# Joining the first and sixth block products of a half pair to 512 columns, and ordering each joined slot

## What is computed

```python
D_MODEL = 2048; SEQ = 512; DIFF_HEADS = 8; DIFF_QK_DIM = 128; DIFF_V_DIM = 256

def diff_attention(u, w_in, w_out, lam_q1, lam_k1, lam_q2, lam_k2, subln_g, rel_table, layer_idx):
    proj = u @ w_in                                   # 512 x 2048 by 2048 x 8192: q | k | v | z
    q = split_heads(proj[..., :E], 2 * DIFF_HEADS)
    k = split_heads(proj[..., E:2 * E], 2 * DIFF_HEADS)
    v = split_heads(proj[..., 2 * E:3 * E], DIFF_HEADS)
    z = proj[..., 3 * E:4 * E]
    ...
    logits = q k^T * scale + rel_bias, causal
    p = softmax(logits);  a = p[:, :, 0] - lam * p[:, :, 1];  o = a v
    o = rms_norm(o, subln_g) * (1.0 - lam_init)
    return (o * silu(z)) @ w_out

h = layer_norm(alpha * x + diff_attention(x, ...), g, b)
```

## Time and profile before

| | us |
|---|---|
| median of 3 runs | 882.47 |
| lowest and highest | 881.83 and 882.64 |
| the profiled execution, device time | 882.91 |
| its span in the trace | 881.1 |

### The profile page before, as it was taken

How to read it: one execution, slowest core, us unless ns; L and a number is a source line. 1 busy time by engine, 2 the same in 40 slices (tenths; PEclk the granted TensorE clock), 3 DMA queues, 4 the chain that set the end, 5 groups by cost and what they waited for, 6 DMA issues and landing times.

```text
span 881.1 us, 15146 instructions
## 1 busy us (share of the span) xinstructions
PE 874.6 (99%) x5498; PEld 792.8 (90%) x5498; DVE 688.1 (78%) x1030; ACT 455.1 (52%) x695; POOL 283.6 (32%) x496
## 2 busy tenths in 40 slices
PE   9999999999999999999999999999999999999997
PEld 7888899999999999999999999999999988888886
DVE  5676778886887788778877887779777976876976
ACT  4445555545555555455545555555455662665511
POOL 1301516152505250525152515250525125130033
PEclk9999999999999999999999999999999999999999
DMA  8822686776677667857785778576857774997723
GB/s 308 312 74 79 142 222 114 225 176 191 126 228 169 179 145 229 162 166 155 232 153 165 163 224 166 156 161 198 166 158 161 259 260 133 232 180 255 286 102 113
DMA packets 54092, 161.38 MB, mean 183 GB/s; under 512 B 9760, under 2 KB 11808, under 8 KB 53808
## 3 DMA queue, kind: packets, MB, share of 16 engines
q0 software_dynamic: 24928, 71.37, 39.6%
q1 hardware_dynamic: 24720, 80.49, 25.9%
q10 hardware_dynamic: 4416, 9.18, 2.9%
HBM read 143.66 MB, written 13.15 MB: 178 GB/s over the span
## 4 chain that ended last, share of the span: by engine, by line
PE 96%; DVE 2%; DMA 0%; ACT 0%; issue 0%; SPq 0%; DVEq 0%; ACTq 0%
PE proj L1736 50%; PE att L1736 46%; DMA w_raw<-w_in_tiles_dram 0%; DVE w_split L1152 0%; DVE w_split L1168 0%; DVE scratch L1320 0%; DVE big L1728 0%; DVE scratch L1347 0%; ACT scratch L893 0%; DVE scratch L1303 0%; DVE xg_split L1465 0%; DVE scratch L1340 0%; DVE last_stats L1714 0%; DVE proj L1254 0%; DVE operands L1298 0%
## 5 line engine op out<-in xcount | busy, mean ns | idle before, releaser
L791 ACT ACTIVATE w_split<-w_raw 128x1024 fp32r<-128x1024 f32 x196 | 207.3, 1058 | 185.8 <-PE proj L1736 115.8
L1152 DVE TENSOR_TENSOR w_split<-w_raw,w_split 128x1024 fp32r<-128x1024 f32 x196 | 238.8, 1221 | 70.8 <-ACT w_split L791 69.7
L1736 PE MATMUL att<-w_split,xg_split 128*128 128x512 f32 x832 | 171.7, 362 | 0.0
L1736 PEld LDWEIGHTS att<-w_split,xg_split 128*128 128x128 f32 x832 | 140.7, 188 | 24.8
L681 POOL DMA_DIRECT2D scratch<-scratch x256 | 127.7, 594 | 41.6 <-DVE scratch L1347 32.2
L1736 PE MATMUL proj<-w_split,xg_split 128*128 128x256 f32 (+1 forms) x912 | 138.5, 311 | 0.1
L1736 PEld LDWEIGHTS proj<-w_split,xg_split 128*128 128x128 f32 x912 | 126.4, 188 | 10.1 <-DVE operands L1298 0.6
L1736 PE MATMUL proj<-xg_split,w_split 128*128 128x256 f32 (+1 forms) x864 | 128.2, 308 | 0.4 <-DVE w_split L1485 0.4
L1736 PEld LDWEIGHTS proj<-xg_split,w_split 128*128 128x128 f32 x864 | 118.3, 189 | 8.7 <-issue 0.7
L704 POOL DMA_DIRECT2D w_raw<-w_in_tiles_dram x84 | 73.9, 887 | 140.2 <-DVE w_split L1152 113.2
L1736 PE MATMUL proj<-w_split,sums 128*128 128x256 f32 (+1 forms) x768 | 104.7, 296 | 0.0
(11 more groups left out here) (188 smaller groups left out, 996.3 us busy)
## 6 DMA issues: line engine op xcount, KB each, us to landing
w_raw<-w_in_tiles_dram SPq DMA_DIRECT2D x98, 512.0 KB, 4.3
w_raw<-w_in_tiles_dram POOLq DMA_DIRECT2D x84, 512.0 KB, 5.5
w_raw<-w_out_tiles_dram SPq DMA_DIRECT2D x19, 512.0 KB, 3.7
w_raw<-w_out_tiles_dram POOLq DMA_DIRECT2D x12, 512.0 KB, 8.0
bias_by_distance<-bias_lines POOLq DMA_DIRECT2D x8, 640.0 KB, 6.2
scratch<-scratch POOLq DMA_DIRECT2D x128, 40.0 KB, 2.8
bias<-bias_by_distance POOLq DMA_DIRECT2D x8, 512.0 KB, 4.2
scratch<-scratch POOLq DMA_DIRECT2D x128, 32.0 KB, 1.7
```

Of the source, the lines that this page charges most:

```text
L791: nc.scalar.activation(split_view(a, 0), pair_raw(a), ACT.Copy).then_inc(w_hi, 1)
L1152: nc.vector.tensor_tensor(split_view(a, 1), pair_raw(a), split_view(a, 0).bitcast(F32), ALU.subtract).then_inc(w_ready, 1)
L1736: return nc.tensor.matmul(dst, lhsT, rhs, start=start, stop=stop, skip_group_check=True)
```

## The change

Steps 0 and 3 are joined too, in both halves. They use both row parts of the two `proj` banks of their column (`half_banks(h, 0)`). ScalarE no longer copies the whole of step 0 but its high-by-low half (`take_first_low`), and VectorE adds the other half to it (`keep_first`). `keep_sum` becomes two additions, the second waiting for the first. Step 6 now opens a sum of its own, so `finish_lower` adds the kept step 0 to it first, and two consumers wait for that. The new ScalarE copy has one more wait, as `kept_first` is now read until the end of a half. In all joined slots, old and new, the eight matmuls of 512 columns are issued first and the eight of 256 after them.

```diff
+        first_low = sem("first_low")
+        sum_begun = sem("sum_begun")
+        upper_left_done = sem("upper_left_done")
...
-        def wide_banks(step):
+        def wide_banks(h, step):
+            if step in (0, 3):
+                return half_banks(h, 0)
             return att[:, WIDE[step]:WIDE[step] + 2].rearrange("p b (l n) -> p b l n", l=2)
...
-            if c == 1:
+            if c == 1 and i in X_ROOM:
                 return xg_split[:, :, X_ROOM[i] + kk, HALF_SEQ:SEQ]
-            low, high, width = k * SEQ + at, D * ST + i * QE + kk * HALF_SEQ, D * ST + 4 * QE
-            return bass.AP(sums, low, [[width, P], [high - low, 2], [1, HALF_SEQ]])
+            low, width = k * SEQ + at, D * ST + 4 * QE
+            if c == 0:
+                high = D * ST + i * QE + kk * HALF_SEQ
+            else:
+                freed = SUM_AT[FREED[i]]
+                high = (2 * SK + SK * (freed % 2) + kk) * SEQ + (HALF_SEQ if freed >= 2 else 0)
+            return bass.AP(sums, min(low, high), [[width, P], [abs(high - low), 2], [1, HALF_SEQ]])
...
-            def keep_first(p, h):
+            def take_first_low(p, h):

                 act.wait_ge(quarter_done, slots_before(p) + h * PHASE + BLOCKS)
-                nc.scalar.activation(kept_first, region_of(h, 0), ACT.Copy).then_inc(first_kept, 1)
+                act.wait_ge(*((v_moved, 2 * p) if h == 0 else (lower_done, phase_number(p, 0) + 1)))
+                nc.scalar.activation(kept_first, wide_banks(h, 0)[:, :, 1], ACT.Copy).then_inc(first_low, 1)
...
             def qk_head(p, e):

                 act.wait_ge(corner_done if e == 1 else lower_done, phase_number(p, 0) + 1)
+                if e == 0:
+                    act.wait_ge(upper_left_done, phase_number(p, 0) + 1)
...
             def v_halves(p):

                 act.wait_ge(scores_done, p * ST + ST)
+                act.wait_ge(upper_left_done, phase_number(p, 1) + 1)
                 act.wait_ge(lower_done, phase_number(p, 1) + 1)
...
-                nc.vector.tensor_tensor(kept_sum, region_of(h, 3), kept_first, ALU.add).then_inc(sum_kept, 1)
+                nc.vector.tensor_tensor(kept_sum, wide_banks(h, 3)[:, :, 0], kept_first, ALU.add).then_inc(sum_begun, 1)
+                dve.wait_ge(sum_begun, n)
+                nc.vector.tensor_tensor(kept_sum, wide_banks(h, 3)[:, :, 1], kept_sum, ALU.add).then_inc(sum_kept, 1)
+
+            def keep_first(p, h):
+
+                dve.wait_ge(first_low, phase_number(p, h) + 1)
+                nc.vector.tensor_tensor(kept_first, wide_banks(h, 0)[:, :, 0], kept_first, ALU.add).then_inc(first_kept, 1)
...
                 dve.wait_ge(lower_begun, phase_number(p, h) + 1)
                 dve.wait_ge(quarter_done, slots_before(p) + (h + 1) * PHASE)
-                nc.vector.tensor_tensor(region_of(h, 5), wide_banks(5)[:, :, 1], kept_sum, ALU.add).then_inc(lower_done, 1)
+                nc.vector.tensor_tensor(region_of(h, 6), region_of(h, 6), kept_first, ALU.add).then_inc(upper_left_done, 1)
+                nc.vector.tensor_tensor(region_of(h, 5), wide_banks(h, 5)[:, :, 1], kept_sum, ALU.add).then_inc(lower_done, 1)
...
                 if j == PHASE:
                     qk_head(p, 0)
+                if r == BLOCKS:
+                    keep_first(p, h)
...
-                opens = c == 0 and (step in (0, 4) or wide)
+                opens = c == 0 and step in (4, 6)
...
+                if wide:
+                    cells = [(group, kk) for group in range(2) for kk in range(SK)]
+                    for group, kk in cells:
+                        part, opening = slice(group * P, (group + 1) * P), c == 0 and kk == 0
+                        dst = wide_banks(h, step)[:, group]
+                        if h == 0:
+                            mm(dst, w[0][:, kk, part], both_x(step, c, kk), opening, False)
+                        else:
+                            mm(dst, xs[0][:, kk, part], both_w[:, :, kk], opening, False)
+                    for group, kk in cells:
+                        part, final = slice(group * P, (group + 1) * P), c == BLOCKS - 1 and kk == SK - 1
+                        dst = wide_banks(h, step)[:, group, 0]
+                        if h == 0:
+                            last = mm(dst, w[1][:, kk, part], xs[0][:, kk], False, final)
+                        else:
+                            last = mm(dst, xs[1][:, kk, part], w[0][:, kk], False, final)
...
-WIDE = {1: 2, 2: 0, 5: 0}
+WIDE = {0: None, 1: 2, 2: 0, 3: None, 5: 0}
```

More of the change, by code:

```diff
@@ L982, in slot @@
                 if r == BLOCKS:
-                    keep_first(p, h)
+                    take_first_low(p, h)
                 late_steps(p - 1, j)
@@ L1211, in keep_sum @@
                 dve.wait_ge(quarter_done, slots_before(p) + h * PHASE + 4 * BLOCKS)
-                nc.vector.tensor_tensor(kept_sum, region_of(h, 3), kept_first, ALU.add).then_inc(sum_kept, 1)
+                nc.vector.tensor_tensor(kept_sum, wide_banks(h, 3)[:, :, 0], kept_first, ALU.add).then_inc(sum_begun, 1)
[4 more added lines that the diff above has]
+                nc.vector.tensor_tensor(kept_first, wide_banks(h, 0)[:, :, 0], kept_first, ALU.add).then_inc(first_kept, 1)
             def keep_third(p, h):
                 dve.wait_ge(third_low, phase_number(p, h) + 1)
-                nc.vector.tensor_tensor(kept_third, wide_banks(1)[:, :, 0], kept_third, ALU.add).then_inc(third_kept, 1)
+                nc.vector.tensor_tensor(kept_third, wide_banks(h, 1)[:, :, 0], kept_third, ALU.add).then_inc(third_kept, 1)
             def keep_fifth(p, h):
                 dve.wait_ge(fifth_low, phase_number(p, h) + 1)
-                nc.vector.tensor_tensor(kept_fifth, wide_banks(2)[:, :, 0], kept_fifth, ALU.add).then_inc(fifth_kept, 1)
+                nc.vector.tensor_tensor(kept_fifth, wide_banks(h, 2)[:, :, 0], kept_fifth, ALU.add).then_inc(fifth_kept, 1)
             def less_sum(p, h):
@@ L1247, in begin_lower @@
                 dve.wait_ge(quarter_done, slots_before(p) + h * PHASE + 6 * BLOCKS)
-                nc.vector.tensor_tensor(kept_sum, wide_banks(5)[:, :, 0], kept_sum, ALU.add).then_inc(lower_begun, 1)
+                nc.vector.tensor_tensor(kept_sum, wide_banks(h, 5)[:, :, 0], kept_sum, ALU.add).then_inc(lower_begun, 1)
             def finish_lower(p, h):
@@ L1855, in product @@
                             last = mm(dst, w[1][:, kk, part], xs[0][:, kk], False, final)
                         else:
-                            mm(dst, xs[0][:, kk, part], w[0][:, kk], first, False)
-                            mm(dst, xs[0][:, kk, part], w[1][:, kk], False, False)
                             last = mm(dst, xs[1][:, kk, part], w[0][:, kk], False, final)
+                else:
+                    for group in range(2):
+                        dst = region_of(h, step)[:, group]
+                        part = slice(group * P, (group + 1) * P)
+                        for kk in range(SK):
+                            first, final = opens and kk == 0, closes and kk == SK - 1
+                            if h == 0:
+                                mm(dst, w[0][:, kk, part], xs[0][:, kk], first, False)
+                                mm(dst, w[0][:, kk, part], xs[1][:, kk], False, False)
+                                last = mm(dst, w[1][:, kk, part], xs[0][:, kk], False, final)
+                            else:
+                                mm(dst, xs[0][:, kk, part], w[0][:, kk], first, False)
+                                mm(dst, xs[0][:, kk, part], w[1][:, kk], False, False)
+                                last = mm(dst, xs[1][:, kk, part], w[0][:, kk], False, final)
```

4 lines of the change are left out of this document (2 added, 2 removed).

## The result

| | before | after |
|---|---|---|
| median, us | 882.24 (4 runs, 881.83 to 882.64) | 876.04 (4 runs, 875.73 to 876.13) |
| profiled run, us (span) | 882.91 (881.1) | 876.08 (874.3) |
| ratio of the medians | | 0.9931, 95% interval 0.9918 to 0.9944 |

The change saves 6.2 us, 0.7%. The forecast was 875.3 us, 0.7 us too low, inside its range and by the mechanism it named. The gain in the loop was forecast an eighth too large (8.54 us, of which the sum counted 8.46, against 7.55), and the experiments show that the reason given for the order's part of it holds for the kernel before and not in general.

What follows compares the result with a forecast made beforehand. The prediction took PE's matmul start rate to bound the loop. Joining 56 slots (5.26 us) and ordering 82 (3.20) gave 8.46, less 1.33 at the last pair's end: 7.13 off the 882.47 median, 875.3 us, range 873.2 to 879.5.

Steps and rivals of the forecast that it cites:

- What bounds the kernel: Loop over the pairs: PE never waits there, so only the rate at which matmuls start sets the time.
- 13.3 ns an instruction, at either width: PE's matmuls: time goes by columns at 2.4 GHz plus 13.3 ns each, 120.0 ns for 256 columns, 226.7 for 512.
- rival D: Joined slots: joining saves nothing, they stay at 2.88 us, only the last pair's end costs; 883.8 us, chance 0.04.
- The price of a wide-first slot: Joined slots, wide matmuls first: 2.773 us plus 0.013 for one turn in each direction, 2.786 us, taken from the weighing of v.
- Alternating the widths thus costs 0.052 us a slot.: Old joined slots: 2.825 us against 2.773 from their matmuls alone, the difference put down to alternating widths.
- VectorE's cover: Added VectorE operations stay off PE's path in the loop; thinnest at slot 0's wait for `z_moved`, margin 0.37 us.
- rival C: Slot 0 waits for `z_moved`: VectorE's chain 0.3 us later than counted, six times, 1.8 us; 877.1 us, chance 0.11.
- Rival E: VectorE becomes the loop's bound at slot 0's wait for `z_moved`, making the kernel slower, up to 902.7 us; chance 0.06.
- The end of the last pair: Chain on VectorE before the output projection: `keep_sum` 0.72 and `finish_lower` 0.61 make it 1.33 us later, bounds 0 to 1.5.
- Rival B: Joined slots: the order brings nothing (2.825 us, total 880.7) or half its effect (2.806, total 878.1); chance 0.14.
- The range: Whole kernel: 873.2 us (both gains at their bounds, end free) to 879.5 (a quarter of the order's effect, 2.815 a slot).

Runs made afterwards that it cites:

- e2: The changed kernel with the old order, widths alternating inside each joined slot, so joining without the order; 876.46 us, ratio to before 0.9936.
- e1: The kernel before with wide matmuls first in the slots it already joins (steps 1, 2 and 5), nothing else; 879.93 us, ratio to before 0.9972.
- e3: The changed kernel with one unused VectorE addition of 128x512 ahead of the z operations in slot 26 of each pair but the last; 879.11 us.
- e7: The changed kernel with two unused VectorE additions of 128x512 ahead of the z operations in slot 26 of each pair but the last; 882.78 us.
- e4: The changed kernel with the last pair's two low splits of weights moved from ahead of `finish_lower` to behind `v_halves`; 874.95 us.
- e11: The kernel before with one unused 256-column matmul at the head of step 1's first slot in each half; 883.74 us, ratio to before 1.0014.
- e10: The kernel before with two unused 256-column matmuls at the head of step 1's first slot in each half; 883.31 us, ratio to before 1.0010.
- e12: The changed kernel with later last-pair splits, step 6 joined, and widths alternating in steps 0 to 3 (first half) and 0 to 2 (second); 876.03 us.
- e9: e4 with widths alternating again in steps 0 to 3 of the first half and 0 to 2 of the second, wide-first elsewhere; 877.95 us.

## Why the prediction was right, step by step

- **What bounds the kernel.** Right. PE had no wait in the loop before or after, and 85 ns for each newly joined slot and 32 for each old one came straight off the time.
- **13.3 ns an instruction, at either width.** Right. e2, which only joins, saves 5.8 us, and its fast slots take 2.773 us, the very sum. That contradicts rival D. The Trainium skill ("TensorE: Matmul & The Clock Gate", section "Back-to-back issue gap") gives the 2.5 ns for an isolated matmul, which the prediction left out; by it the joining would have brought about 1.1 us, an estimate. The section adds that in a stream of weight loads and matmuls this formula counts too much at 512 columns, 216 ns where 131 were measured. Here it counts too little, with 226.7 measured, so neither figure holds for this stream.
- **The price of a wide-first slot.** This is the term that was mis-sized: "one turn in each direction costs 0.013 us", 2.786 us a slot. It is 0.020 and 2.793. The turn to 512 columns costs 27 ns, spread over five matmuls (233 236 228 233 231 against 226.7), the way back gives 7 or 8 ns, once (113). The neighbour was the right one and its rows were too coarse: I had read the turn off two starts rounded to 0.01 us, an error as large as the term. By the starts of its single matmuls the weighing of v takes 2.447 us in the kernel before, 0.020 above 2.427, with the same intervals (233 236 228 233 231 226 227, then 113). 140 slots by 0.007 is 1.0 us: the loop's forecast of 8.54 becomes 7.5, and 7.55 was measured. By kind of slot, the newly joined ones gave 4.80 us of the 5.26 forecast, the old ones 2.69 of 3.28.
- **"Alternating the widths thus costs 0.052 us a slot."** Right for the kernel before, wrong as a property of alternation. In the fast rhythm it costs nothing (2.77). So the order's gain isn't one number: 2.3 us alone (e1), 0.4 us on top of joining (876.46 to 876.04), since joining by itself had moved most of the slots into the fast rhythm. A sum of separate gains, as I made it, hit the total only because the order puts the joined slots at 2.793 whatever was before. That the two gains added up was luck: the prediction had no row for an alternating stream with steps 0 and 3 joined.
- **VectorE's cover.** Right. z's operations end 0.39 us ahead of slot 0 (forecast 0.37), and slot 3's weights have 3.0 us of slack where 2.8 were forecast. The timeline of VectorE over the end of pair 3, where the slot starts at 353.86:
```profile
352.20 1.27 DVE L1325 SCALAR_TENSOR_TENSOR scratch<-scratch,proj 128x512 f32<-128x512 f32 x2
353.40 1.21 DVE L1166 TENSOR_TENSOR w_split<-w_raw,w_split 128x1024 fp32r<-128x1024 f32 x1
```
  I had said that the handover comes off this margin without its size. It is 0.24 with the weight load, so rival C was closer than its chance of 0.11 told: one more operation in the wrong place costs 3.1 us (e3), two the whole gain (e7). Rival E is a real mechanism, with its edge 0.15 us away.
- **The end of the last pair.** Right: forecast 1.33, and 0.08 by which PE arrives earlier, measured 1.40. `finish_lower` and `keep_sum` lie there as worked out; e4 shows that it needn't be paid.
- **Rival B**, that the order brings only a part of its gain, is true by a fifth: 0.007 of 0.039.
- **The range.** Its upper end is stated as 879.5. Worked out as written (2.815 us a slot, 1.33 at the end) it is 879.3; 879.5 needs the 1.5 us of the end's own bound.

## What to carry to other kernels

Where PE never waits, read its time off the starts of matmuls, over hundreds of one kind and not over one short run, and price the turn between two kinds from single intervals before it is multiplied by 140. Put two changes of a stream to the test one at a time and together: here they bring 2.3 and 5.8 us alone and 6.2 together. Before an engine off the path gets more work, take the handover (0.24 us here) from the margin, since behind the edge each added microsecond counts whole, every time round the loop.

## What the hardware showed that I had not expected

An alternating stream of 512- and 256-column matmuls, with no wait in it, runs in one of two lasting rhythms: 353 ns a pair of matmuls (2.825 us a slot) or 347 (2.77), 2% apart, at the same granted clock. It keeps the one it has from slot to slot, up to seven in a row in e2. Whether one or two narrow matmuls are put ahead of it decides (2.82 us in e11, 2.77 in e10), and a short stand seems to do so too (e12). Wide matmuls in a block of eight, then the narrow ones, take 2.793 us a slot behind plain and behind other wide-first slots. Directly behind an alternating slot one took 2.775 (slot 20 of e9). What in PE holds the phase stays open: the records show starts and not the stages within PE, and the link between the last narrow interval (124 ns) and the fast rhythm is an observation over these kernels, tested by e10, e11 and e9, and no mechanism.
